# A mixture-of-experts decoder layer: expert rows weighted on their way out and added by the gathering DMA, gate and up weights one row to a packet

## The chip, the cores and the metric

The kernel runs on one core of one Trainium2 chip. The metric is device time in microseconds from one launch to its end. A profiled execution also gives a span, from its first to its last instruction. Everything is float32 at the interface; products are formed from two float32r parts (a rounded value and what the rounding left), in three matmuls each.

## The reference, cut to what matters

520 tokens (512 of a prompt, 8 samples) of 1024 numbers pass one layer: three convolution and gating branches, an output projection and a layer norm give `h`; then each token goes to two of 16 experts, and a second layer norm follows.

```python
def moe_ffn(h, ...):                     # 16 experts in 4 groups, the 2 best of the best group
    weights = sel_v / jnp.sum(sel_v, axis=-1, keepdims=True)
    gates = ...                          # (tokens, 16), two entries of each row not zero
    for e in range(N_EXPERTS):
        u = jax.nn.silu(t @ w_gate[e]) * (t @ w_up[e])      # (n,1024) @ (1024,512)
        out = out + gates[:, e:e + 1] * (u @ w_down[e])     # (n,512) @ (512,1024)
    return out.reshape(n, L, d)

f = moe_ffn(h, ...)
y = layer_norm(ALPHA * h + f, ln2_g, ln2_b)
```

The kernel divides by ALPHA throughout: it sums `h` and the two expert rows with weights over ALPHA, and takes the epsilon of the norm over ALPHA squared.

## The kernel before, in words

**Token mixer, 0 to 684 us.** `project` (L1079) multiplies 128-column blocks of weights, loaded 512 KB at a time (`raw`, L425) and split by ScalarE (L724) and GpSimd (L595). At the very start SyncE's queue loads inputs in a fixed order; `sb_tok`, the old state of a convolution, comes in at L439, and TensorE turns it at L1056 before it goes on.

**Opening of the experts, 684 to 733 us.** VectorE makes `h_tok` (L1712), SyncE stores it to `h_rows` in HBM, VectorE finds the two experts of each token and its place in the list of each. For an expert, `mark` (L1794) makes a one-hot matrix of tokens by places, `find_ids` (L1234) multiplies it with the token numbers, `take_ids` (L1801) makes them integers, GpSimd gathers up to 96 rows of `h_rows` into `hs` (L632), TensorE turns them (`turn`, L1245), ScalarE and VectorE make `hs_hi` (L891) and `hs_lo` (L1806). While the first gather runs TensorE turns the identity 18 times, and 8 times after the first `turn` (`keep_busy`, L1227).

**The expert stage, 733 to 988 us.** One step per expert, 16 in all, those of 1 to 12 in a hardware loop. Weights have three slots (expert e, e+1, e+2), 2 MB for each of gate, up and down. In a step TensorE does the gate product (24 matmuls of 512 columns), `find_ids` for the expert after the next, `turn_u`, `turn`, the up product (24) and the down product of the expert before (24), into `work[1]`. ScalarE rounds each of the 12 chunks into a ring of six, VectorE subtracts (`low_parts`, L1705). ScalarE's order in a step: up chunks, two down chunks, silu, `u_hi`, `hs_hi`, two down chunks, four gate chunks, and at the end `rows_out` (L900): it copies `work[1]` to `y_out` once the down product is done and the store of the last `y_out` has landed. VectorE's order: up chunks 0 and 1, `mark`, up 2 and 3, down 0 and 1, `take_ids`, `u_lo`, `hs_lo`, down 2 and 3, gate 0 and 1, `u`, gate 2 and 3. SyncE's queue issues, each after what it overwrites is used: gate of e+3, up of e+3, down of e+2 (all L474), and the store of `y_out` to `y_rows` (L483). All four go through one queue (q1) in this order; the gather of `hs` goes through GpSimd's (q0).

In HBM a row of gate or up is 512 floats, 2 KB. The view of before gives each partition two neighbouring rows (`e (j p i) f`, i=2), so that 4 KB are contiguous; the rows of the contraction are thereby paired, and `h_tok` is written with its columns in paired order (views `paired` and `plain`), `turn` takes its 128-column blocks in the order 0, 4, 1, 5, ..., and later sums with `h_back` go through the same views. Down has rows of 4 KB.

**The end, 960 to 1027.7 us.** In steps 13 and 14 VectorE works out at which row of `y_rows` the two results of each token lie (`find_slots`, `order_slots`, L1916 to L1935), the earlier-stored one first (`slot_early`, clipped to the first 12 experts). Once the down product of step 14 is done SyncE loads `h` back into `h_back`, and GpSimd gathers the earlier rows into `y_a` (L677). The last expert is split in halves (`up_last` L1289, `down_last` L1302). VectorE then spreads the samples' row numbers over the partitions (`spread_samples`, L1942 and L1943), makes the shares of the last expert (`share_marks`, L1952 to L1961) and forms `y_a*weight + h_back` (`partial`, L1967) for each of four token blocks and the samples. GpSimd gathers the later rows into `y_b` (`slot_ready`). The last expert's rows don't go through HBM for the prompt: TensorE adds identity times `y_a` (L1385) and three products of the weighted shares with the last rows (L1387) in PSUM. VectorE adds `y_b*weight` (L2006), with ScalarE (square, root, scale; L981, L984, L988) and GpSimd (add of the bias; L712) it normalises block after block, the samples between blocks 2 and 1, and five stores bring the results out.

GpSimd's queue at the end: four early gathers, the samples' early gather (after L1943), four late gathers (after L1961), the samples' late gather (after the last rows are stored), three bias adds.

Of the kernel before, what the change touches and what calls it, by code (L numbers as in the profile page):

```python
# [22 lines left out]
F32 = mybir.dt.float32  # L23
F32R = mybir.dt.float32r
BF16 = mybir.dt.bfloat16
I32 = mybir.dt.int32
# [90 lines left out]
def build(nc, x_prompt, x_sample, state_conv_a, state_conv_b, w_in, conv_a_w, w_a_out, conv_b_w, conv_b_bias,  # L117
# [4 lines left out]
    y_rows = nc.dram_tensor("y_rows", (PASSES * E * C, D), F32, kind="Internal").ap()  # L122
# [7 lines left out]
    gate_v = expert_w_gate[0].rearrange("e (j p i) f -> p (e j) (i f)", p=P, i=2)  # L130
    up_v = expert_w_up[0].rearrange("e (j p i) f -> p (e j) (i f)", p=P, i=2)
    down_v = expert_w_down[0].rearrange("e (k p) n -> p (e k) n", p=P)

    with ExitStack() as ctx:
# [103 lines left out]
        s_own, s_spread, s_idx = sb("s_own", [TS, 5]), sb("s_spread", [P, 5]), sb("s_idx", [P, 3], I32)  # L238
# [16 lines left out]
        share_tok = place("share_tok", "Q_HI", [P, 4, C], plus=NTB * D * 4)  # L255
        share_hi = place("share_hi", "Q_HI", [C, 4 * P], F32R, plus=NTB * D * 4 + 4 * C * 4)
        share_lo = place("share_lo", "Q_HI", [C, 4 * P], F32R, plus=NTB * D * 4 + 4 * C * 4 + 4 * P * 4)
        block_mean = place("block_mean", "acc_a", [P, P], plus=960)
        spread = place("spread", "acc_a", [TS, P], plus=960 + P * 4)
# [6 lines left out]
        onehot = place("onehot", "acc_a", [P, NTB, C], BF16)  # L266
# [9 lines left out]
        agg = sb("agg", [P, 2, 4])  # L276
        assert cursor[0] <= nc.sbuf_usable_end - 64, (cursor[0], nc.sbuf_usable_end)
# [47 lines left out]
        y_a_in, y_b_in = [sem(f"y_a_in{b}") for b in range(NTB)], [sem(f"y_b_in{b}") for b in range(NTB)]  # L325
        partial_ready = sem("partial_ready")
# [7 lines left out]
        class Pass:  # L334


            def __init__(self, tag):
                self.onehot_ready, self.ids_mm, self.ids_ready = sem(tag + "onehot"), sem(tag + "ids_mm"), sem(tag + "ids_ready")
                self.gathered = sem(tag + "gathered")
                self.turned, self.hs_hi_ready, self.hs_lo_ready = sem(tag + "turned"), sem(tag + "hs_hi"), sem(tag + "hs_lo")  # L340
# [44 lines left out]
        plain = lambda t: t.rearrange("p (g i) -> p i g", i=2)  # L385
        paired = lambda t: t.rearrange("p (i g) -> p i g", i=2)
        plain_s = lambda t: t.rearrange("p (x i) -> p i x", i=2)
        paired_s = lambda t: t.rearrange("p (i x) -> p i x", i=2)
        z_tile = (pr[0], work[1], pr[1], work[0])
        wide = lambda t: t.rearrange("p (h n) -> p h n", h=2)  # L390
        sz_in, sz = pr[0][:, 0, CS:2 * CS], pr[0][:, 0, 0:CS]
# [24 lines left out]
        def _(sp):  # L416
# [21 lines left out]
            load(0, N_S1 + 2, in_v, s1_roles[2])  # L438
            sp.dma_start(sb_tok[:], state_conv_b[0].rearrange("(b s) k n -> (s k) b n", b=2)).then_inc(states_in, 16)  # L439
# [30 lines left out]
            views = {"gate": (gate_v, KB // 2), "up": (up_v, KB // 2), "down": (down_v, FB)}  # L470
# [10 lines left out]
            def store(ps, e, t, row0):  # L481
                sp.wait_ge(ps.y_ready, t + 2)
                sp.dma_start(y_rows[bass.ds(e * C + row0, C), :], y_out[:]).then_inc(ps.stored, 16)  # L483

            def load_back():

                sp.dma_start(h_back[:, 0:4, :], h_rows[0:TP, :].rearrange("(b p) n -> p b n", p=P)).then_inc(back_in, 16)
                for i in range(2):
                    sp.dma_start(sh_back[:, i * (CS // 2):(i + 1) * (CS // 2)],
                                 h_rows[TP:T, :].rearrange("s (i c x) -> i s c x", i=2, x=CS // 2)[i]).then_inc(back_in, 16)  # L490
# [60 lines left out]
            with sp.If(n_max > C):  # L551
                sp.wait_ge(first.stored, 16 * E)
                sp.wait_ge(first.half_stored, 32)
                sp.wait_ge(partial_ready, NTB)
# [25 lines left out]
        def _(pool):  # L580
# [30 lines left out]
            pool.iota(e_off[:].rearrange("p b (g i) -> p b g i", i=PER_GROUP), pattern=[[0, NTB], [C, GROUPS], [GROUPS * C, PER_GROUP]], base=0, channel_multiplier=0, allow_small_or_imprecise_dtypes=True)  # L611
# [42 lines left out]
            pool.wait_ge(h_stored, 16 * NTB)  # L654
# [20 lines left out]
            def fetch(dst, slot, landed, table):  # L675
                for b in range(4):
                    pool.indirect_dma_start(out=dst[:, b, :], out_offset=None, in_=table,  # L677
                                            in_offset=bass.IndirectOffsetOnAxis(ap=slot[:, b:b + 1], axis=0)).then_inc(landed[b], 16)

            def fetch_samples(dst, which, landed, table):  # L680

                pool.indirect_dma_start(out=dst, out_offset=None, in_=table.rearrange("r (c f) -> (r c) f", f=CS),
                                        in_offset=bass.IndirectOffsetOnAxis(ap=s_idx[:, which:which + 1], axis=0)).then_inc(landed[4], 16)
# [6 lines left out]
            fetch_samples(sy_a, 0, y_a_in, y_rows[0:EARLY * C, :])  # L690
            n_max = further_passes(pool)
            with pool.If(n_max > C):
# [7 lines left out]
                fetch(y_a, slot_a, y_a_in, y_rows)  # L700
                fetch_samples(sy_a, 1, y_a_in, y_rows)
                fetch(y_b, slot_b, y_b_in, y_rows)
                fetch_samples(sy_b, 2, y_b_in, y_rows)
            with pool.Else():
                pool.wait_ge(slots_ready, 4)
                pool.wait_ge(first.stored, 16 * E)
                fetch(y_b, slot_ready, y_b_in, y_rows[0:(E - 1) * C, :])
                pool.wait_ge(first.half_stored, 32)
                fetch_samples(sy_b, 2, y_b_in, y_rows[0:E * C, :])
# [1391 lines left out]
```

## Time and profile before

| | us |
|---|---|
| three runs, median (lowest, highest) | 1028.82 (1028.72, 1029.62) |
| profiled execution | 1029.47 |
| its span | 1027.7 |
| TensorE busy in it | 999.9 (97%) |
| VectorE busy | 793.4 (77%) |
| ScalarE busy | 478.5 (47%) |
| GpSimd busy | 379.0 (37%) |
| mean granted TensorE clock | 0.993 |

Busy is the time in which an engine had an instruction in flight. A busy TensorE is not one at its peak, since matmuls are pipelined. The chain of waits goes back from the last instruction, at each step to what released it. DMA share is the time that the packets of the 16 DMA engines took, over 16 times the stretch; queues are SyncE's (q1), ScalarE's (q10) and GpSimd's (q0).

### The profile page before, as it was taken

Reading aid. Unit: us, or ns where it says so; the run is one execution under the profiler, and the core shown is the slowest. Engines: PE = TensorE matmul, PEld = TensorE weight load, DVE = VectorE, ACT = ScalarE, POOL = GpSimd, SP = SyncE. Lnnn points to the kernel's source line nnn. Section 1 sums busy time; section 2 is a strip of 40 time slices with the busy share of each in tenths; the row PEclk is TensorE's granted clock in tenths of the full one; section 3 lists DMA queues with packets and bytes.
Section 4 is the critical chain, followed back from the end, with each engine's and each line's share of the span. In section 5 each row is a group of like instructions: output and inputs, shape, how many; then the busy total and the mean of one; then the engine's idle time right before and its main releaser. Section 6 shows DMA issues by size and latency. Waiting matters only on the chain.

```text
span 1027.7 us, 19645 instructions
## 1 busy us (share of the span) xinstructions
PE 999.9 (97%) x7246; PEld 904.1 (88%) x7246; DVE 793.4 (77%) x982; ACT 478.5 (47%) x674; POOL 379.0 (37%) x278
## 2 busy tenths in 40 slices
PE   7999999999999999999999999998999999999995
PEld 7999999999999999999999999986677777777773
DVE  4598889888989985844434498237989898999987
ACT  4232322223232335134442323452788887878765
POOL 3444444444454755344544454320200000000355
PEclk9999999999999999999999999998999999999998
DMA  7432323233232222333235522647999999999475
GB/s 219 120 103 82 102 82 97 86 88 95 85 99 82 82 83 73 101 111 91 82 102 162 186 82 92 257 154 286 398 389 397 391 399 389 399 391 399 155 247 179
DMA packets 147290, 190.55 MB, mean 185 GB/s; under 512 B 6819, under 2 KB 114339, under 8 KB 147228
## 3 DMA queue, kind: packets, MB, share of 16 engines
q1 hardware_dynamic: 140107, 176.74, 49.4%
q0 software_dynamic: 3008, 10.55, 3.2%
q10 hardware_dynamic: 4129, 2.67, 0.9%
q8 instruction: 26, 0.43, 0.2%
q14 instruction: 20, 0.16, 0.1%
HBM read 179.16 MB, written 11.76 MB: 186 GB/s over the span
## 4 chain that ended last, share of the span: by engine, by line
PE 91%; DVE 5%; issue 2%; DMA 2%; ACT 1%; POOL 0%; SPq 0%; DVEq 0%; POOLq 0%; ACTq 0%
PE pr L1079 60%; PE pr L1269 16%; PE work L1269 8%; DMA sb_tok<-in_state_conv_b_dram 1%; PE work L1245 1%; PE work L1161 1%; PE pr L1310 1%; PE pr L1289 1%; DMA hs<-h_rows,ids 0%; PE work L1186 0%; DVE y_a L2015 0%; PE work L1087 0%; PE pr L1234 0%; DVE q_hi L1596 0%; PE pr L1178 0%
## 5 line engine op out<-in xcount | busy, mean ns | idle before, releaser
L595 POOL TENSOR_TENSOR w_lo<-raw,w_hi 128x512 fp32r<-128x512 f32 x208 | 297.2, 1449 | 326.8 <-ACT w_hi L724 326.8
L1079 PE MATMUL pr<-x_hi,w_hi 128*128 128x260 f32 x1264 | 255.2, 283 | 0.0
L1079 PE MATMUL pr<-x_hi,w_lo 128*128 128x260 f32 x1264 | 254.8, 283 | 0.0
L1079 PE MATMUL pr<-x_lo,w_hi 128*128 128x260 f32 x1264 | 254.3, 283 | 0.0
L728 ACT ACTIVATE ev<-pr 128x520 f32<-128x520 f32 x96 | 58.2, 606 | 372.7 <-PE pr L1079 372.7
L1079 PEld LDWEIGHTS pr<-x_hi,w_hi 128*128 128x128 f32 x1264 | 195.0, 189 | 0.3
L1079 PEld LDWEIGHTS pr<-x_hi,w_lo 128*128 128x128 f32 x1264 | 194.9, 188 | 0.0
L1079 PEld LDWEIGHTS pr<-x_lo,w_hi 128*128 128x128 f32 x1264 | 194.3, 188 | 0.0
L1522 DVE SCALAR_TENSOR_TENSOR work<-b_pad,par,work 128x512 f32<-128x512 f32 x224 | 148.1, 742 | 0.0
L724 ACT ACTIVATE w_hi<-raw 128x512 fp32r<-128x512 f32 x208 | 118.9, 622 | 3.7 <-DMA raw<-in_w_in_dram 3.4
L632 POOL DMA_INDIRECT hs<-h_rows,ids x15 | 19.3, 1288 | 247.5 <-DVE ids L1801 247.5
L1269 PE MATMUL pr<-ring,hs_hi 128*96 128x512 f32 x246 | 97.8, 398 | 0.0
L1269 PE MATMUL pr<-ring,hs_lo 128*96 128x512 f32 x246 | 96.8, 393 | 0.0
L1705 DVE TENSOR_TENSOR w_up_lo<-w_up,ring 128x1024 fp32r<-128x1024 f32 x64 | 75.2, 1219 | 19.0 <-ACT ring L868 19.0
L868 ACT ACTIVATE ring<-w_gate 128x1024 fp32r<-128x1024 f32 x64 | 67.8, 1062 | 23.3 <-PE pr L1269 10.6
L1705 DVE TENSOR_TENSOR w_down_lo<-w_down,ring 128x1024 fp32r<-128x1024 f32 x64 | 75.3, 1214 | 1.7 <-ACT ring L868 1.7
L1705 DVE TENSOR_TENSOR w_gate_lo<-w_gate,ring 128x1024 fp32r<-128x1024 f32 x64 | 75.4, 1215 | 0.8 <-ACT ring L868 0.7
L1582 DVE TENSOR_TENSOR ev<-ev,ev 128x520 f32<-128x520 f32 x16 | 11.9, 744 | 79.4 <-ACT ev L728 79.4
L868 ACT ACTIVATE ring<-w_down 128x1024 fp32r<-128x1024 f32 x64 | 65.7, 1053 | 4.7 <-PE pr L1269 4.0
L868 ACT ACTIVATE ring<-w_up 128x1024 fp32r<-128x1024 f32 x64 | 62.4, 1046 | 2.1 <-PE pr L1261 1.9
L1269 PEld LDWEIGHTS pr<-ring,hs_lo 128*96 128x96 f32 x246 | 39.7, 161 | 17.3
L1269 PEld LDWEIGHTS pr<-ring,hs_hi 128*96 128x96 f32 x246 | 39.8, 162 | 16.0
(397 smaller groups left out, 1749.7 us busy)
## 6 DMA issues: line engine op xcount, KB each, us to landing
raw<-in_w_in_dram SPq DMA_DIRECT2D x80, 512.0 KB, 3.7
w_gate<-in_expert_w_gate_dram SPq DMA_DIRECT2D x16, 2048.0 KB, 14.4
w_up<-in_expert_w_up_dram SPq DMA_DIRECT2D x16, 2048.0 KB, 13.0
w_down<-in_expert_w_down_dram SPq DMA_DIRECT2D x16, 2048.0 KB, 12.5
y_rows<-y_out SPq DMA_DIRECT2D x14, 384.0 KB
raw<-in_w_a_out_dram SPq DMA_DIRECT2D x8, 512.0 KB, 4.1
raw<-in_w_c_out_dram SPq DMA_DIRECT2D x8, 512.0 KB, 4.1
raw<-in_w_b_out_dram SPq DMA_DIRECT2D x8, 512.0 KB, 3.9
```

Of the source, the lines that this page charges most:

```text
L595: pool.tensor_tensor(w_lo[:, slot, k], raw[:, slot, k], w_hi[:, slot, k].bitcast(F32), ALU.subtract).then_inc(w_split, 1)
L632: pool.indirect_dma_start(out=hs[:], out_offset=None, in_=h_rows, in_offset=bass.IndirectOffsetOnAxis(ap=ids[:, m % 2:m % 2 + 1], axis=0)) ...
L724: act.activation(w_hi[:, slot, k], raw[:, slot, k], ACT.Copy).then_inc(w_rounded, 1)
L728: act.activation(out, src[:, :, 0:HALF], func).then_inc(evacuated, 1)
L868: act.activation(rounded(kind, i, last, opening, slots), chunk(kind, s, i), ACT.Copy).then_inc(ps.hi[kind], 1)
L1079: mm = pe.matmul(pr[slot][:, h, 0:HALF], w[:, slot, k, :], x[:, k, h * HALF:(h + 1) * HALF], start=(k == 0 and w is w_hi and x is hi), sto ...
L1161: mm = pe.matmul(work[TILE[f"sp{q}"]][:, i, c * P:(c + 1) * P], vt[:, c, g * P:(g + 1) * P], ws_t[:, g, :], start=True, stop=True)
L1245: mm = pe.transpose(work[0][:, k // 4, k % 4 * C:(k % 4 + 1) * C], source[:, (k % 2 * 4 + k // 2) * P:(k % 2 * 4 + k // 2 + 1) * P], ident ...
L1269: mm = pe.matmul(out(h), x[:, k, :], w[:, cols], start=(k == 0 and x is hi and w is w_hi_i), stop=(k == k_of * CH - 1 and x is lo))
L1522: do(dve.scalar_tensor_tensor(acc, b_pad[:, k:k + TP], col(j, R_CONVB + k), acc, ALU.mult, ALU.add))
L1582: do(dve.tensor_tensor(gate[:], gate[:], prod[:], ALU.mult))
L1705: dve.tensor_tensor(chunk(kind, s, i, w_e_lo), chunk(kind, s, i), rounded(kind, i, last, opening, slots).bitcast(F32), ALU.subtract).then_ ...
```

## The change

Five things are done together.

1. **Weights.** Gate and up are viewed as down is, one 2 KB row to a packet. `h_tok`, `turn` and the load of `h_back` go back to plain column order; the instructions stay as many.
2. **Gated rows.** Three more bf16 columns beside the token numbers hold each token's weight for each expert in three parts (`slot_cols`, made by the new `spread_weights` from nine small VectorE operations). `find_ids` multiplies five columns in place of two, from a place that a register gives. ScalarE sums the three parts of the gate into `gate` (`gate_in`), for the first two experts ahead of the first `hs_hi` (`first_gates`, after ten matmuls `find_gates` that take the place of the eight turns of the identity), for the others between `hs_hi` and down chunk 2 (`next_gate`, which waits for `take_ids`). `rows_out` and `last_rows_out` scale by it. `onehot` has two buffers.
3. **Adding gathers.** Both gathers of each block go straight into `h_back`, with the DMA adding; the early ones wait for the load of `h_back`, a late one for the early one of its block. A row of zeros (row 0 of `y_rows`, stored at the start behind the third weight load, ahead of `sb_tok`) serves where nothing is to be added. `partial`, `sample_partial` and a copy of the samples on ScalarE are gone.
4. **Shares.** They are plain ones and zeros: `share_marks` is one VectorE operation in step 14, the four turns stand in step 15 ahead of `up_last`, ScalarE copies them once (before the store of expert 14's rows), and `share_last` has two matmuls per half block in place of four. The low part of the last rows is made with the gate as a factor, and `y_last` is copied after it.
5. **Order.** `spread_samples` comes before the last chunk of `low_parts`; `order_slots` loses ten small operations and gains three (one clips, one multiplies, one makes `slot_ready`); the ScalarE root that loads a table moves behind the branch for further passes.

```diff
-    gate_v = expert_w_gate[0].rearrange("e (j p i) f -> p (e j) (i f)", p=P, i=2)
-    up_v = expert_w_up[0].rearrange("e (j p i) f -> p (e j) (i f)", p=P, i=2)
+    gate_v = expert_w_gate[0].rearrange("e (k p) f -> p (e k) f", p=P)
+    up_v = expert_w_up[0].rearrange("e (k p) f -> p (e k) f", p=P)
@@ SyncE, start
             load(0, N_S1 + 2, in_v, s1_roles[2])
+            sp.wait_ge(x_split, 1)
+            sp.dma_start(y_rows[0:1, :]..., b_pad[0:1, 0:16]...to_broadcast([1, D // 16, 16])).then_inc(h_stored, 16)
             sp.dma_start(sb_tok[:], ...).then_inc(states_in, 16)
@@ GpSimd, end
+            def fetch(b, slot, table):
+                pool.indirect_dma_start(out=h_back[:, b, :], out_offset=None, in_=table,
+                                        in_offset=..., compute_op=ALU.add).then_inc(y_in[b], 16)
             pool.wait_ge(slots_ready, 3)
             pool.wait_ge(first.stored, 16 * (EARLY + 1))
-            pool.wait_ge(first.done["down"], (E - 1) * CH)
-            fetch(y_a, slot_early, y_a_in, y_rows[0:EARLY * C, :])
-            pool.wait_ge(end_dve, 2)
+            pool.wait_ge(back_in, 32)
+            for b in range(4):
+                fetch(b, slot_early, y_rows[0:EARLY * C + 1, :])
+            pool.wait_ge(end_dve, 3)
...
                 pool.wait_ge(first.stored, 16 * E)
-                fetch(y_b, slot_ready, y_b_in, y_rows[0:(E - 1) * C, :])
+                for b in range(4):
+                    pool.wait_ge(y_in[b], 16)
+                    fetch(b, slot_ready, y_rows[0:(E - 1) * C + 1, :])
+                pool.wait_ge(y_in[4], 16)
                 pool.wait_ge(first.half_stored, 32)
@@ ScalarE
+            def gate_in(ps, src, m):
+                act.activation(gate_parts[:, m % 2], src, ACT.Copy, accum_out=gate[:, m % 6:m % 6 + 1]).then_inc(ps.gates_in, 1)
+            def next_gate(ps, m, t):
+                act.wait_ge(ps.ids_ready, t + 4)
+                act.wait_ge(ps.gates_in, t + 2)
...
-            def rows_out(ps, t):
+            def rows_out(ps, m, t):
                 act.wait_ge(ps.done["down"], t * CH + 2 * CH)
                 act.wait_ge(ps.stored, t * 16 + 16)
+                act.wait_ge(ps.gates_in, t + 1)
-                act.activation(y_out[:]..., work[1][0:C], ACT.Copy).then_inc(ps.y_ready, 1)
+                act.activation(y_out[:]..., work[1][0:C], ACT.Copy, scale=gate[:, m % 6:m % 6 + 1]).then_inc(ps.y_ready, 1)
@@ TensorE
                 turn(ps, n0)
-                if ps is first:
-                    keep_busy(8)
+                find_gates(ps, n0)
...
-                    pe.matmul(z_tile[b][:, h, :], ident[:], y_a[:, b, cols], start=True, stop=False)
-                    for w, y in ((share_hi, y_last_hi), (share_lo, y_last_hi), (share_hi, y_last_lo)):
+                    for y in (y_last_hi, y_last_lo):
@@ VectorE, end
-                    spread_samples()
-                    share_marks()
-                    partials(16)
+                    share_low(0)
+                    share_low(1)
```

## Rows read from the trace of the kernel before

**Rows 1.** The page: the chain of waits, shares of the span.

```profile
PE 91%; DVE 5%; issue 2%; DMA 2%; ACT 1%; POOL 0%; SPq 0%; DVEq 0%; POOLq 0%; ACTq 0%
```

**Rows 2.** A step: stretch, us, PE PEld DVE ACT POOL busy, clock, DMA share, GB/s.

```profile
930.00:948.00 18.00, 18.00 (x94) 12.95 (x93) 16.41 (x18) 14.67 (x17) 0.92 (x1) 1.00 1.03 396
```

**Rows 3.** DMA queues, 720 to 945 us: packets, MB, share of 16 engines.

```profile
q1 hardware_dynamic: 21161, 83.47, 95.0%
```

**Rows 4.** The same of 420 to 540 us, where rows are 512 B.

```profile
q1 hardware_dynamic: 20840, 11.47, 31.8%
```

**Rows 5.** The same of 1001 to 1007 us: two stores of 2 KB rows.

```profile
q10 hardware_dynamic: 224, 0.39, 19.8%
```

**Rows 6.** DMA issues, 745 to 762 and 923 to 941: KB, us to landing.

```profile
w_gate<-in_expert_w_gate_dram SPq DMA_DIRECT2D x1, 2048.0 KB, 14.4
...
w_gate<-in_expert_w_gate_dram SPq DMA_DIRECT2D x1, 2048.0 KB, 14.9
```

**Rows 7.** Tile y_rows: DMA to landing, us.

```profile
DMA to landing us min/median/max: 2.1/5.7/12.1
```

**Rows 8.** Timeline, SyncE and ScalarE: start us, us [idle before <-releaser].

```profile
942.76 0.36 SPq L483 DMA_DIRECT2D y_rows<-y_out  x1
...
959.35 1.03 ACT L900 ACTIVATE y_out<-work 96x1024 f32<-96x1024 f32 x1 [1.70 <-PE work L1269]
```

**Rows 9.** Timeline of one step, VectorE and TensorE.

```profile
785.03 0.65 DVE L1794 TENSOR_TENSOR onehot<-ev,router 128x480 bf16<-128x480 f32 x1
786.01 0.34 PE L1234 MATMUL pr<-id_cols,onehot 128*96 128x2 bf16 x5
790.14 0.15 DVE L1801 TENSOR_REDUCE ids<-pr 96x1 int32<-96x2 f32 x1
```

**Rows 10.** The chain of waits at the start: start us, us, what.

```profile
15.22 0.39 SPq L425
15.65 11.39 DMA sb_tok<-in_state_conv_b_dram
```

**Rows 11.** Timeline of the opening, TensorE, ScalarE, VectorE.

```profile
711.96 1.14 PE L1245 MATMUL work<-ident,hs 96*128 96x96 f32 x8 [0.24 <-DMA hs<-h_rows,ids]
713.14 0.81 ACT L891 ACTIVATE hs_hi<-work 128x768 fp32r<-128x768 f32 x1 [8.51 <-PE work L1245]
714.00 0.48 PE L1257 MATMUL pr<-ring,hs_hi 128*96 128x512 f32 x1
708.91 0.16 DVE L1801 TENSOR_REDUCE ids<-pr 96x1 int32<-96x2 f32 x1
```

**Rows 12.** Timeline of ScalarE: a small operation that sums.

```profile
1016.31 0.31 ACT L1001 ACTIVATE y_b<-pr,s_agg 128x64 f32<-128x64 f32 x1
1016.52 0.19 ACT L1001 ACTIVATION_READ_ACCUMULATOR y_b<-pr,s_agg 128x1 f32 x1
```

**Rows 13.** Timeline of the end, VectorE.

```profile
1000.39 0.17 DVE L1961 CAST slot_ready<-s_pos 128x5 int32<-128x5 f32 x1
1006.76 1.29 DVE L2006 SCALAR_TENSOR_TENSOR pr<-y_b,s,pr 128x1024 f32<-128x1024 f32 x1 [0.82 <-PE pr L1387]
1008.22 1.27 DVE L1967 SCALAR_TENSOR_TENSOR y_a<-y_a,s,h_back 128x1024 f32<-128x1024 f32 x1
1014.44 0.29 DVE L2038 SCALAR_TENSOR_TENSOR pr<-y_b,s_spread,pr 128x64 f32<-128x64 f32 x1
```

**Rows 14.** Timeline of the end, ScalarE and its queue: the last rows.

```profile
1002.55 0.58 ACT L912 ACTIVATE y_last_hi<-work 96x512 fp32r<-96x512 f32 x1
1002.68 0.32 ACTq L914 DMA_DIRECT2D y_rows<-y_last  x1
```

**Rows 15.** Timeline of the end, GpSimd's gathers of the later rows.

```profile
1000.83 1.74 POOL L677 DMA_INDIRECT y_b<-y_rows,slot_ready  x1 [0.82 <-DVE slot_ready L1961]
1008.30 2.02 POOL L682 DMA_INDIRECT y_b<-y_rows,s_idx  x1 [0.30 <-issue]
```

**Rows 16.** Tile slot_ready: DMA to landing, us.

```profile
DMA to landing us min/median/max: 5.5/5.7/5.9
```

More of the change, by code:

```diff
@@ L265, in build @@
         u_lo = place("u_lo", "par", [P, FB, C], F32R)
-        onehot = place("onehot", "acc_a", [P, NTB, C], BF16)
+        onehot = [place(f"onehot{i}", "acc_a", [P, NTB, C], BF16, plus=i * NTB * C * 2) for i in range(2)]
+        slot_cols = place("slot_cols", "rw", [P, NTB, E, 5], BF16)
         iota = ev[4][:, 0:C]
@@ L553, in _ @@
                 sp.wait_ge(first.half_stored, 32)
-                sp.wait_ge(partial_ready, NTB)
+                for b in range(NTB):
+                    sp.wait_ge(y_in[b], 16)
                 sp.wait_ge(end_mm, 6)
@@ L699, in _ @@
                 pool.wait_ge(y_read, 1)
[L700 to L703, printed above, removed]
+                pool.wait_ge(back_in, 64)
+                for b in range(4):
+                    fetch(b, slot_a, y_rows)
+                fetch_samples(1, y_rows)
+                for b in range(4):
+                    pool.wait_ge(y_in[b], 32)
+                    fetch(b, slot_b, y_rows)
+                pool.wait_ge(y_in[4], 32)
+                fetch_samples(2, y_rows)
             with pool.Else():
@@ L940, in step @@
                         rounded_parts(ps, "up", s, uses[s] + m // 3, t, slots="down")
-                        rows_out(ps, t - 1)
+                        rows_out(ps, m - 1, t - 1)
+                        if ps is first:
+                            act.wait_ge(end_mm, 1)
+                            act.activation(share[:], pr[1][0:C, 1, :], ACT.Copy).then_inc(end_act, 1)
                         return
@@ L1342, in step @@
                         down(ps, (m - 1) % 3, t - 1, slots="up")
+                        if ps is first:
+                            pe.wait_ge(end_dve, 2)
+                            for b in range(4):
+                                mm = pe.transpose(pr[1][0:C, 1, b * P:(b + 1) * P], share_tok[:, b, :], ident[:])
+                            mm.then_inc(end_mm, 1)
                         pe.wait_ge(ps.u_ready, t * 2 + 2)
@@ L1351, in step @@
                     if m <= 13:
-                        find_ids(ps, t + 2)
+                        find_ids(ps, m, t + 2, expert(2))
                     if m:
@@ L1838, in expert_pass @@
                 take_ids(ps, 1, n0 + 1)
+                if ps is first:
+                    spread_weights()
                 if ps is further:
```

282 lines of the change are left out of this document (128 added, 154 removed).

## The prediction

> **What bounds the kernel now.** First the page's chain of waits: TensorE's own work is 91% of the span [rows 1], so what does not reach TensorE costs nothing until the end. Then the busy time by stretch: an expert's step takes 17.9 us, TensorE has no gap in it, ScalarE 3.3 us and VectorE 1.6 us of 18; the DMA engines have none either, 396 GB/s at a share of 1.03 [rows 2]. So two resources are full at the same pace. That the DMA engines are just at their limit shows in the landings: gate loads take 14.4 us from issue to landing at 745 us and 14.9 at 923 [rows 6], though 2 MB at 396 GB/s are 5.3; the queue is never empty and its backlog grows a little. Third, the cover: gate, up and down are loaded two to three steps ahead, some 38 us between issue and use against 15, so they may be late by 20 us. The store of `y_out` stands in the same queue behind them, and its cover is short: issued at 942.76, it has to have landed when ScalarE writes the next `y_out` at 959.35 [rows 8], 16.6 us later. Of the landings that the view shows for `y_rows` the longest is 12.1 us [rows 7]; I take it for a store of this stage. 16.6 - 12.1 leaves 4.5 us. Last, the chain at the start goes through the load of `sb_tok` [rows 10], in the opening through the first gather, the turn, `hs_hi` and then TensorE without a pause [rows 11], and at the end through VectorE.
>
> **Weights in 2 KB packets.** As many bytes in twice the packets: 2 MB in 1024 in place of 512. What a packet costs: in the expert stage 16 x 225 us x 0.950 / 21161 = 161.6 ns at a mean of 3945 B [rows 3]; in the mixer 16 x 120 x 0.318 / 20840 = 29.3 ns at 550 B [rows 4]. The line through both is 7.8 ns + 0.039 ns per byte: 2 KB cost 88 ns, twice that is 175 against 167 for 4 KB. A load has 512 more packets on 16 engines, 32 each, 0.25 us. The only 2 KB packets in the trace are two stores beside gathers: 16 x 6 x 0.198 / 192 = 99 ns (the 224 hold 32 completion writes) [rows 5]; by them a load would cost 32 x (2 x 99 - 167) = 1.0 us more. The bounds are 0 and 1.0; I take 0.30, by the line, since loads are its kind, with a little for packets that meet others. Steps issue no slower, so the backlog grows by 0.60 us a step. From the moment the queue was last empty (713.9) to the store at 942.76 there are 26 loads of gate or up: 7.8 us. The cover takes 4.5, passed after some 15 loads, in step 8. From there on `y_out` waits for its store, and behind it on ScalarE stand the up chunks, behind those on VectorE `mark`, and for that TensorE's `find_ids` waits: `mark` ends at 785.68 and TensorE begins at 786.01 [rows 9], a cover of 0.3. So the last steps run at the pace of the DMA engines, and the stage ends 7.8 - 4.5 - 0.3 = 3.0 us later. With 0.16 per load or less nothing shows; with 0.45 it is 6.9; a cost of 1.0 would give 21, which I don't reach for, since a write beside gathers is the farther row.
>
> The Trainium skill, "DMA: Bandwidth & Descriptors", section Specifications, puts the least transfer for line rate at 512 B; by this 2 KB would cost what 4 KB do per byte. The trace disagrees at 512 B: 29.3 ns for 550 B is 301 GB/s over 16 engines, 161.6 for 3945 is 391 [rows 3, 4]. By the rule this term would be 0 and the sum 1029.0; that is the first rival below.
>
> **Gates in the steps.** `find_ids` has as many matmuls, three columns wider: 0.34 us as now. It takes its place from a register, which adds sequencer instructions to TensorE; no row shows their cost there. They run ahead under 5.5 us of products unless `mark` is late; bounds 0 and 0.1 a step (12 steps, 1.2 us), taken 0. `next_gate` on ScalarE costs an operation and a read of the sum: 16.52 - 16.31 + 0.19 = 0.4 us [rows 12], and it waits for `take_ids`, done at 790.29 [rows 9]; behind it stand two down chunks and four gate chunks, with 3.3 us of ScalarE's slack in the step [rows 2], and VectorE behind those with 1.6. They are used by TensorE 3 us later or more, so 0. The scale from a tile in `rows_out` adds some 0.1 us in the tight loop of `mark`; taken 0, it is in the 0.3 above.
>
> **Start.** SyncE issues one more DMA before `sb_tok`; one costs its queue 0.39 us and 0.04 between [rows 10], and `x_split` has long come. `sb_tok` is waited for by TensorE from its landing at 27.04 on, after which TensorE never waits in the mixer: +0.4 us (0, if the DMA engines, loaded then, hide it, to 0.8).
>
> **Opening.** `first_gates` stands ahead of the first `hs_hi`, which began 0.04 us after the turn, and TensorE began 0.05 us after that [rows 11]. New before it: ten small matmuls, 2 x 0.18 = 0.35 us (five of them span 0.34 with their tail [rows 9]), and two gate sums, 2 x 0.4 = 0.8 [rows 12]. `spread_weights` has nine small operations, some 2.5 us from 709.07, and is done before the turn ends at 713.1. The eight turns of the identity ran beside `hs_hi` and free nothing. +1.1 us, 0.8 to 1.6; TensorE paces what follows, so it stays.
>
> **End.** Gone from VectorE: three partials before the last products and, between the first two sums, the fourth (1.27 us [rows 13]) and the samples' (0.3). Gone from TensorE: eight identity products and a third of the others; the first sum waited 0.82 us for TensorE at 1006.76 [rows 13]. `slot_ready` no longer comes last, at 1000.39 [rows 13]; instead the late gathers wait behind the samples' early one, whose row numbers come at about 998.5, so the first is issued at 1000.0 in place of 1000.83 [rows 15]. At 5.7 us to landing [rows 16] the first sum begins at 1005.7, 1.0 earlier, and the second 2.6 earlier. Against this: the four turns of shares ahead of `up_last` (0.35), ScalarE's copy of them ahead of the down chunks (0.6), for which VectorE was already waiting, and `spread_samples` ahead of the last chunk (0.3) push the last rows back by 1.2; the second half no longer waits for the shares and gains as much. But each half is now rounded (0.58 [rows 14]), waits for its low part, and is then copied: its store goes out at about 1004.3 in place of 1002.68 [rows 14]. It lands near 1008, and only then may the samples' late gather be issued, as late as now, 1008.30 [rows 15]. It lands at 1012 to 1014 (4 to 5.7 us after). Before it stand the first three sums, done by 1011.7, and behind it blocks 1 and 2 and the sum of block 3. That sum was at 1014.44 [rows 13] and comes at 1012.5: -1.9 us, if an adding gather is as fast as a copying one. If an adding packet takes twice the time, a gather of 512 KB takes 2.6 us of all engines in place of 1.3, the four late ones land at 1006.4, 1009, 1011.6 and 1014.2, the samples after them at 1014.9, and the end comes 0.5 later than now. No row shows an adding DMA. Bounds -2.5 and +2; I take -1.1, between the two, as nothing is near.
>
> The Trainium skill, same page, section "Rules for kernel authors", says that an accumulating DMA reads its destination and writes it later. No run here shows it; that is the doubled case, by which the end would be +0.5 in place of -1.1 and the sum 1.6 us higher.
>
> **Sum.** 3.0 + 0 + 0.4 + 1.1 - 1.1 = +3.4 us on a profiled execution of 1029.47, which lay 0.65 above the median. On the median of 1028.82 that is 1032.2.
>
> **Rivals.**
> - *The backlog stays hidden; not slower.* A load costs 0.16 us more or less, or the growth is taken up as loads of the queue are issued later. For it: a packet's own cost is the smaller part of 88 ns, and mean packet times at a share of 1.03 hold queueing. Against: landings grow already [rows 6], so no room is left. Then 0 + 0.4 + 1.1 - 1.1: 1029.2.
> - *The end gives more, and the backlog is hidden; faster.* The mechanism is VectorE's chain at the end: the samples' gather lands by 1011.5, adding costs nothing, and all of 1.0 + 1.5 us is kept. It decides if that gather lands before the third sum ends. 1028.82 + 1.5 - 2.8 = 1027.5, and 1026.4 if the opening costs but half.
> - *Adding gathers are dear.* Late gathers queue behind each other at 2.6 us and VectorE waits for each. 3.0 + 1.5 + 0.5 to 2: 1033.8 to 1035.3. For it: two early gathers of a block in a row, each reading what it adds to. Against: the engines are nearly idle at the end.
> - *Packets are dearer.* 0.45 us a load: 6.9 in place of 3.0, 1036.1.
> - *The change doesn't do what it says*, the 2 KB rows being joined to larger packets: then it is the first rival.
>
> **How the numbers follow.** Forecast 0.37, its own range 1030.9 to 1034; backlog hidden 0.22 (about no change); faster end 0.16; dear gathers 0.13; dear packets 0.12. The range leaves out the ends of the last two and a part of the third: 1026.8 to 1036. A measurement here tells 0.2%, 2.1 us, from no change: faster means below 1026.8, 0.15; within, to 1030.9, 0.30; slower 0.55.
>
> **What would show it.** Right: in the expert stage packets of q1 double in number at 85 to 95 ns; landings of gate loads grow from about 15 us to over 20 and `y_out` gets an idle time released by a DMA in the last third, while steps go from 17.9 to 18.4 us there. `sb_tok` issued at 16.1; the first product of the experts 1.1 us further from the turn. At the end VectorE waits before the samples' sum. Wrong: steps of 17.9 us throughout with the store's landing under 16 us, or steps of over 18.4 from the start of the stage; a step that waits for `find_ids` or `hs_lo` with the store long landed; gathers that land later than 8 us after issue.

## The result, and the profile after

The changed kernel takes 1042.78 us (median of 4 runs, 1041.97 to 1044.09) against 1029.22 for the kernel before beside it; the ratio is 1.0133, 95% interval 1.0115 to 1.0150. It is 13.6 us slower; the forecast was +3.4, its range ended at +7.2. The profiled run took 1041.97 (span 1040.1).

Both traces are cut at three marks that every kernel here has: VectorE's last `m` of the mixer, TensorE's turn of `u` in step 1 and in step 15, and the end of VectorE's last operation. Each number is a difference of start times in the chain of waits or the timeline.

| stretch | before | after | |
|---|---|---|---|
| start to the end of the mixer | 683.37 | 682.41 | -1.0 |
| opening, to the turn of `u` in step 1 | 49.31 | 51.49 | +2.2 |
| steps, to the turn of `u` in step 15 | 247.05 | 251.93 | +4.9 |
| end, to VectorE's last operation | 43.77 | 51.54 | +7.8 |

That is 13.9; the spans differ by 12.4, as the last stores behind that mark took 1.5 less.

**Steps.** The chain of waits of the kernel after, in step 2 of the loop and in step 13, which stands outside it and takes its columns from a fixed address (start us, us, what):

```profile
751.66 0.56 PE pr L1263 x5
752.22 0.46 PE pr L1348 x4
...
953.12 0.19 PE pr L1263 x5
953.31 0.39 PE pr L1348 x4
```

And what stands in TensorE's queues for that line in the whole stage (ns min/median/max):

```profile
L1263 PEldq FUSED_REGOPS  x60: 46/46/84, 733.1 to 935.0; - x60
```

L1263 is `find_ids`. In the loop its five products take 0.50 to 0.56 us and the turn of `u` behind them 0.46; outside, with the same five columns, 0.19 and 0.39. That is some 0.43 us in each of the twelve steps whose address comes from a register, and steps of 18.31 us in place of 17.88. The 60 register operations are one to a product, 5 in each of the 12 steps; in the step above they start from 751.3 to 751.9 us, among the weight loads of the five products, which span 0.67 us there and 0.41 in step 13. So they are not done ahead, under the products before. The stretch of a step, the DMA queue of 720 to 945 us and what ScalarE waits for before it writes `y_out` (all 15 times TensorE), beside [rows 2, 3, 8]:

```profile
930.00:948.00 18.00, 18.00 (x89) 12.92 (x88) 16.31 (x17) 14.23 (x19) 0.92 (x1) 1.00 1.04 386
```
```profile
q1 hardware_dynamic: 33314, 81.41, 96.6%
```
```profile
  PE work L1307: 26.9, 15
```

Packets grew from 21161 to 33314, and GB/s fell from 396 to 386, but `y_out` never waited for its store: the forecast's main term did not appear. The slower steps gave the DMA engines the time they needed; e1 below bears that out.

**Opening.** The chain, and the granted clock of three stretches (its column stands third from the end), against [rows 11]:

```profile
710.99 0.88 PE work L1283 x8
711.87 0.42 PE pr L1272 x10
...
712.32 0.41 ACT gate_parts L905 x4
712.73 0.71 ACT hs_hi L898
...
713.48 0.74 PE pr L1295
714.22 0.43 PE pr L1296
```
```profile
711.00:713.00 2.00, 1.28 (x18) 1.19 (x18) 0.00 (x0) 0.68 (x5) 0.00 (x0) 1.00 0.19 76
713.00:715.00 2.00, 1.52 (x4) 1.07 (x5) 1.54 (x2) 0.43 (x1) 0.00 (x0) 0.52 0.59 74
715.00:717.00 2.00, 2.00 (x7) 1.30 (x6) 2.00 (x3) 0.54 (x1) 0.00 (x0) 0.62 0.97 352
```

`find_gates` and the gate sums stand in the chain as forecast. Behind `find_gates` TensorE was idle from 712.3 to 713.5, and then the granted clock fell to the level of 1.2 GHz: the first products take 0.43 us each, and 0.23 where it is 2.4.

**End.** GpSimd's gathers, VectorE, and ScalarE around its branch, against [rows 13 to 16] (start us, us, engine line, operation, [idle before <- releaser]):

```profile
994.72 2.39 POOL L675 DMA_INDIRECT h_back<-y_rows,slot_early  x1 [30.96 <-DMA h_back<-h_rows]
...
1006.80 1.54 POOL L675 DMA_INDIRECT h_back<-y_rows,slot_ready  x1 [0.30 <-issue]
...
1019.46 1.55 POOL L680 DMA_INDIRECT h_back<-y_rows,s_idx  x1 [5.57 <-DMA y_rows<-y_last]
```
```profile
1015.90 1.23 DVE L2015 SCALAR_TENSOR_TENSOR pr<-pr,h_back 128x1024 f32<-128x1024 f32 x1 [5.62 <-DMA h_back<-y_rows,slot_ready]
...
1030.93 1.23 DVE L2048 SCALAR_TENSOR_TENSOR y_b<-h_back,s_agg 128x64 f32<-128x64 f32 x1
...
1032.26 2.19 DVE L2051 SCALAR_TENSOR_TENSOR y_a<-y_b,s_agg,h_back 128x64 f32<-128x64 f32 x1
1034.38 1.28 DVE L2023 SCALAR_TENSOR_TENSOR work<-work,agg,ln_rows 128x1024 f32<-128x1024 f32 x1
```
```profile
1011.04 0.32 ACTq L938 DMA_DIRECT2D y_rows<-y_last  x1
1020.84 1.28 ACT L1049 ACT_TABLE_LOAD   x1 [9.83 <-issue]
```

And the DMA queues and landings of 1003 to 1018 us:

```profile
q0 software_dynamic: 843, 2.58, 93.8%
...
y_rows<-y_last ACTq DMA_DIRECT2D x2, 192.0 KB, 7.3
h_back<-y_rows,slot_ready POOLq DMA_INDIRECT x4, 10.6
```

Three things to see. The late gathers land after 10.6 us in place of 5.7, with the DMA engines full at only 200 GB/s. ScalarE issues nothing for 9.8 us around its branch (2.9 before). Two operations of VectorE on 64 columns take 1.23 and 2.19 us. The forecast had the first as its doubled case, worth 1.6 us; the other two had no term.

Which of them paces the end is in the chain of waits (start us, us, what):

```profile
1010.32 0.69 ACT y_last L936
...
1013.70 7.14 issue
1020.84 1.28 ACT L1049
...
1023.54 1.29 DVE y_a L2023
```

It goes from the last rows over ScalarE's branch to its first square, and from there along VectorE; no gather stands in it. The first square starts 36.4 us after the turn of `u` in step 15, 29.1 before: with the 2.0 us of the two operations (e6) that is more than the whole loss. So in the changed kernel the adding gathers wait in the shadow of the branch, and come out once that is repaired (e5, e8).

### The profile page after: what moved, and what is told of

Same layout as the page of the kernel before. It is cut to its first block, busy times and chain, and to the rows that moved or that the text cites. A ratio compares the mean times of both kernels' runs of the same rounds, so it can differ in the third digit from the quotient of the medians.

```text
span 1040.1 us, 19719 instructions
## 1 busy us (share of the span) xinstructions
PE 997.2 (96%) x7224; PEld 903.7 (87%) x7224; DVE 791.7 (76%) x969; ACT 476.6 (46%) x703; POOL 366.4 (35%) x278
## 4 chain that ended last, share of the span: by engine, by line
PE 91%; DVE 4%; issue 3%; ACT 1%; DMA 0%; ACTq 0%; POOL 0%; DVEq 0%; POOLq 0%
PE pr L1107 60%; PE pr L1307 16%; PE work L1307 8%; PE work L1283 1%; PE pr L1263 1%; PE work L1189 1%; PE pr L1348 1%; PE pr L1126 1%; PE pr L1327 1%; DMA hs<-h_rows,ids 0%; PE work L1214 0%; DVE y_a L2023 0%; PE work L1115 0%; DVE q_hi L1634 0%; PE pr L1206 0%
## 5 line engine op out<-in xcount | busy, mean ns | idle before, releaser
L631 POOL DMA_INDIRECT hs<-h_rows,ids x15 | 13.9, 929 | 260.1 <-DVE ids L1852 247.0
```

The costliest lines, as they stand in the source:

```text
L631: pool.indirect_dma_start(out=hs[:], out_offset=None, in_=h_rows, in_offset=bass.IndirectOffsetOnAxis(ap=ids[:, m % 2:m % 2 + 1], axis=0)) ...
```

## The experiments

Times are medians; the kernel before lay at 1028.6 to 1029.0 beside them. A median carries some scatter of the start: the end of the mixer lies between 682.4 and 683.5 in the profiles, but at 685.6 in those of e1 and e5, where TensorE waited 1.8 and 1.7 us for `sb_tok` (0.7 before, at most 1.3 in the other kernels) and its first 16 products behind it took 2.4 and 2.6 us in place of 1.9 (granted clock 0.65 and then 0.50 from 28 to 31 us in e5). So what each experiment shows is read by stretch. The end scatters too: e1 and e7 change nothing in it and have 49.4 and 50.0 against the 51.5 of after. That is the gap at ScalarE's branch: its first square starts 34.2 and 34.9 us after the turn of `u` in place of 36.4, and the ends are shorter by just that. So there a difference of 2 us says nothing by itself, and the place is read in the trace:

| kernel | time | opening | steps | end |
|---|---|---|---|---|
| before | 1028.7 | 49.31 | 247.05 | 43.77 |
| after | 1042.8 | 51.49 | 251.93 | 51.54 |
| e1 fixed tile of columns | 1037.1 | 50.37 | 247.46 | 49.36 |
| e2 before, 2 KB packets | 1030.5 | 49.04 | 247.55 | 43.89 |
| e3 gathers that copy | 1039.3 | 50.43 | 252.26 | 48.98 |
| e4 root ahead of the branch | 1041.6 | 50.49 | 252.25 | 50.04 |
| e5 branch turned round | 1042.6 | 50.57 | 251.76 | 48.58 |
| e6 samples in PSUM | 1041.4 | 51.89 | 251.91 | 48.38 |
| e7 gate sums late | 1040.0 | 49.80 | 251.85 | 50.02 |
| e8 = e1, e5, e6, e7 | 1033.8 | 49.46 | 247.35 | 48.08 |
| e9 = e8, late gathers copy | 1031.2 | 50.52 | 248.71 | 43.25 |
| e10 = e9, 4 KB, strided turn | 1033.8 | 50.19 | 251.44 | 42.79 |

(In e7, e9 and e10 the turn of step 15 is not in the chain and is taken from the timeline.)

**e1: is it the register?**

```
+ dve.tensor_copy(cols_now[:, m % 2], slot_cols[:, :, bass.ds(x, 1), :]...)      # in mark
- of = slot_cols[:, b, bass.ds(x, 1), :]                                         # in find_ids
+ of = cols_now[:, m % 2, b, :]
```

> After, but VectorE copies the five columns of the expert to a fixed tile beside each mark, and TensorE reads that tile instead of an address from a register. Theory (the register addresses cost TensorE its 0.43 us a step): find_ids back from some 0.5 to 0.2 us in the chain of waits, looped steps from 18.31 to about 17.9, the time 4 to 5.5 us under the changed kernel's 1042.8, so 1037 to 1039. Rival A (the steps are paced by the DMA engines, which move 2 KB packets): steps stay at 18.3, 1042.8. Rival B (the wider product, five columns for two, costs): find_ids stays at 0.5. A mixture that I keep open: steps are 17.9 at first and longer in the last third, where y_out waits for its store, as forecast: then 1040 to 1041.

1037.08 (1036.36 to 1038.90). The chain of the same step:

```profile
753.63 0.19 PE pr L1266 x5
753.82 0.39 PE pr L1351 x4
754.20 0.66 PE work L1286 x8
```

Five columns from a fixed address take 0.19 us, and the steps 4.5 us less. The register address is shown as the cause; width and DMA are ruled out. The time is at the lower end of what was expected. The mixture came too, smaller: `y_out` waited five times for its store and two late steps were 17.97 and 18.05 us.

**e2: the packets alone.** The kernel before, with the two views and their counts changed. It leaves out the plain column order of the tokens that goes with them, so its output is another; the work is the same:

```
- "e (j p i) f -> p (e j) (i f)", i=2
+ "e (k p) f -> p (e k) f"
```

> Before, with only the gate and up matrices loaded one 2 KB row to a packet (the rows then meet the wrong columns of the tokens, the work is the same). The recorded term: 0.30 us a load, backlog of 7.8 us by step 14, stage 3.0 us longer, so 1032.2. Rival A (a packet of 2 KB costs half of one of 4 KB, or the queue has more cover than I counted): no change, 1029.2 and steps of 17.88 to the end. Rival B (packets dearer): 1036.

1030.47 (10 runs, 1029.28 to 1032.76), ratio 1.0016, interval 1.0006 to 1.0025. What `y_out` waits for and how its store lands, and one piece of the chain of waits:

```profile
  PE work L1269: 15.6, 9
  DMA y_rows<-y_out: 12.5, 6
...
DMA to landing us min/median/max: 3.2/15.7/16.3
```
```profile
925.26 16.29 DMA y_rows<-y_out
```

The mechanism is the one forecast: the landing grows step by step (13.0, 13.6, 14.5, 15.0, 15.8 us for the first five stores), stops at about 16 when it meets the cover, and from 869 us on, in step 8, ScalarE waits for the store, which stands in the chain from 925. But it costs 0.5 us in the steps, 1.7 by the medians (the profiled execution, 1029.28, was the fastest of the ten), not 3.0. The queue q1 held 33550 packets at 97.2% of 225 us, 104.3 ns each; less some 7650 of 4 KB (12.6 steps of 512 and 96) at the 161.6 ns of [rows 3], a 2 KB packet took 87 to 88 ns. That is the 88 of the forecast's line; what the forecast added above it ("a little for packets that meet others") was not there. By 32 x (2 x 87.5 - 167) = 0.26 us a load the forecast's own sum gives 26 x 0.26 - 4.8 = 2.0 us, still four times the 0.5 of the trace; what holds the rest back is not shown.

**e3: is adding dear?** The ten gathers overwrite, which leaves `h` and the earlier rows out of the sums:

```
- ..., compute_op=ALU.add)
+ ...)
```

> After, with the ten gathers of rows overwriting in place of adding (the sums then lack the residual and the early rows; all else the same). Theory (adding is dear for the DMA engines, some twice a copy): late gathers land 5.5 to 6 us after issue in place of 10.6, the DMA engines are under a share of 0.6 from 1003 to 1023, the first sum starts 4 us earlier, and ScalarE's gap of 9.4 us at the branch falls to about 3 as before, since what it waits for there comes over the same DMA engines; 1042.8 less 3 to 5: 1038 to 1040. Rival (the gap at the branch comes from the place of the square root's table load): gap unchanged, end 0 to 2 us earlier.

1039.27 (1038.42 to 1040.59). The same 15 us:

```profile
q0 software_dynamic: 781, 2.73, 54.9%
...
h_back<-y_rows,slot_ready POOLq DMA_INDIRECT x4, 6.4
```

The first sum starts at 1011.25 in place of 1015.90. Per packet 16 x 15 x 0.549 / 781 = 169 ns where adding took 16 x 15 x 0.938 / 843 = 267; from 1013 to 1015 us the engines moved 371 GB/s at a share of 0.94, the adding ones 217 at 1.07. Adding is shown as dear. The Trainium skill, "DMA: Bandwidth & Descriptors", section "Rules for kernel authors", has an accumulating DMA read its destination and write it later; the trace fits it, with little over half the rate. The part on ScalarE's gap fell: it is 7.3 us here (9.8 after), so most of it is not the adding, and VectorE, its sums done early, waits 5.6 us (3.1 after) for ScalarE's first square. That starts 2.6 us nearer to the turn of `u`, which is all that the end is shorter by: on the chain of the changed kernel the adding costs nothing beyond what it may add to the gap.

**e4 and e5: the gap at the branch.** e4 puts `act.activation(r_tok..., Sqrt)` ahead of it; e5 turns it round:

```
- with act.If(n_max > C): <further passes>
- with act.Else(): act.nop()
- <root>; normalised()
+ with act.If(n_max < C + 1): <root>; normalised()
+ with act.Else(): <further passes>; <root>; normalised()
```

> After, with ScalarE's small Sqrt that loads the table put back ahead of the branch. Theory of contention: the branch still takes its 7 us beside the adding gathers, what follows it comes 0 to 1.3 us earlier; 1042.8 less 0 to 1.3. Rival (the table load behind the branch is what waits, or brings the wait about): ScalarE's Square starts 5 us or more earlier than 1022.3, VectorE's normalise(0) loses its wait of 3.1 us; 1040 to 1041.

> After, with ScalarE's branch turned round: what follows it in this input (root and normalising) stands directly behind the branch, the code of the further passes behind that. Theory (the 6 to 7 us between the branch and the next instruction are the fetch of instructions from a far place, over the DMA engines that are busy with the gathers): the gap falls from 7.1 to under 2 us, ScalarE's first Square comes 5 us earlier, VectorE no longer waits 3.1 us for it; the time 1.5 to 3 us under 1042.8. Rival (the branch waits for the value it loads, or for anything that comes wherever the code stands): gap and time unchanged.

e4: 1041.57 (1040.46 to 1043.64), 1.2 less as contention allows, but within the scatter; the root's table load came at 1011.39, a gap of 5.7 us stood behind the root, and the first square started 2.4 us earlier, not the 5 of the rival. e5: 1042.58 (1041.40 to 1043.34), ScalarE first, then the chain of waits:

```profile
1013.09 0.32 ACTq L938 DMA_DIRECT2D y_rows<-y_last  x1
1014.56 1.28 ACT L1042 ACT_TABLE_LOAD   x1 [1.50 <-issue]
```
```profile
1013.09 7.89 DMA y_rows<-y_last
...
1021.73 4.14 DMA h_back<-y_rows,s_idx
```

The gap went from 9.8 to 1.5 us with nothing changed but the order of the code: it belongs to the jump over the further passes. The traces speak for instructions fetched by the DMA engines: two queues of the kind `instruction` (q8 and q14) move packets of 16 KB and less, and in each of the eight long gaps (before, after, e1 to e4, e6, e7) at least one of them does, the last some 1 to 2 us before the gap ends (after: at 1019.4, the gap to 1020.8; before: at 1005.9, to 1007.5). In the gaps of 1.0 to 1.6 us of e5, e8, e9 and e10 there is none. The gap was also longer where the DMA engines were busier (2.9 us before, 7.3 in e3, 9.8 after). That these packets are ScalarE's instructions no view says. VectorE's wait of 3.1 us for ScalarE's first square is gone, yet the time missed what was expected, 1.5 to 3 us less. In the profiled execution the end is 3.0 us shorter and the mixer ended 3.2 later; where the three others lost it isn't known. At the end the next chain comes out: the store of the last rows, 7.9 us to landing, and the samples' gather behind it.

**e6: VectorE behind GpSimd.**

```
+ act.activation(sz, sh_back, ACT.Copy)                      # sz, sz_out: PSUM
- scalar_tensor_tensor(sy_b, sh_back, ...); scalar_tensor_tensor(sy_a, sy_b, ...)
+ scalar_tensor_tensor(sz_out, sz, ...);    scalar_tensor_tensor(sy_a, sz_out, ...)
```

> After, with the samples' two last VectorE operations reading their first operand from PSUM (a copy that ScalarE makes) in place of SBUF. Theory (VectorE, with both operands in SBUF, is held until GpSimd's running addition ends): the operations of 128x64 fall from 1.23 and 2.19 us to 0.3 each, as before, and the last normalising starts 2.9 us earlier, less what ScalarE's own chain for block 3 allows; 1042.8 less 1.5 to 3. Rival (the operations are long for another reason, as the memory of h_back or the DMAs): unchanged.

1041.36 (1040.82 to 1043.53):

```profile
1030.83 0.28 DVE L2050 SCALAR_TENSOR_TENSOR pr<-pr,s_agg,h_back 128x64 f32<-128x64 f32 x1
...
1031.21 0.28 DVE L2053 SCALAR_TENSOR_TENSOR y_a<-pr,s_agg,h_back 128x64 f32<-128x64 f32 x1
1032.25 1.29 DVE L2025 SCALAR_TENSOR_TENSOR work<-work,agg,ln_rows 128x1024 f32<-128x1024 f32 x1 [0.76 <-ACT y_b L1012]
```

Shown. In the kernel after, GpSimd's first two additions ran from 1026.36 for 2.35 us and from 1029.72 for 2.36, the next followed; VectorE's operations ended at 1032.16 and 1034.45, when the second and the third addition did. The Trainium skill, "SBUF — State Buffer", section "Who interferes with whom", says that a VectorE instruction with two SBUF inputs contends with a GpSimd instruction that reads SBUF, and calls the lock on the shared ports exclusive. The trace agrees, 0.28 against 1.23 and 2.19 us. From the first of the two to the last normalising it is 1.42 us in place of 3.45, so 2.0 of the expected 2.9, as ScalarE's `y_b` then ends last. The time, 1.4 less, is just short of the 1.5 to 3 expected.

**e7: the gate sums.** `first_gates` moves from ahead of step 0 to behind `tokens_in(ps, 0, t)`.

> After, with the two first gate sums of ScalarE behind hs_hi in place of ahead of it. Theory (they stand on the chain of the opening): the first product comes 0.41 us (the part of them that the chain shows) to 0.8 us nearer to the turn, the time 0.4 to 0.8 less, 1042.0 to 1042.4, in the profile and hardly beyond what a median tells. Rival: TensorE's clock decides there: the granted clock falls where TensorE has a long pause before the first product, and the time moves by 1.2 either way.

1040.04 (1038.82 to 1041.02). The chain:

```profile
711.19 1.01 PE work L1283 x8
...
712.22 0.82 ACT hs_hi L898
...
713.08 0.47 PE pr L1295
```

The time is 2.7 less, beyond the 0.4 to 0.8 expected. The opening is 1.7 us shorter than after's: the gates' 0.7 (as e3 and e4, whose clock stayed up, stand to it) and 1.0 of a granted clock that is 1.00 from 713 on; the end, which this edit leaves alone, is 1.5 shorter, as the gap at ScalarE's branch is. The clock fell behind the pause in after and e6 (1.2 us) and in e9 (0.5), and not in e1, e3, e4 and e5 (1.2) nor in e7 and e8 (0.5); what decides isn't settled, so the 1.0 is not something that this edit is shown to give back. Another 0.4 of the opening is step 1's `find_ids`.

**e8: together.**

> After with the fixed tile of columns, the branch turned round, the samples' operands in PSUM and the late gate sums together. If the parts add up: 1042.8 - 5.7 - 2 - 2.5 - 0.5 = 1032. If they share one chain at the end (the store of the last rows, 7.2 us to landing, then the samples' gather, 5.6 us, both beside adding gathers), the two at the end give 2 together and it is 1034.5.

1033.80 (1031.86 to 1034.83): between the two values expected, 0.7 below the one of a shared chain. Opening and steps are as before, and the end is still 4.3 us longer, on one chain:

```profile
1004.66 8.79 DMA y_rows<-y_last
...
1014.20 4.23 DMA h_back<-y_rows,s_idx
```

The late gathers are close behind that chain: VectorE waits 5.4 and 2.5 us for them ahead of its first two sums, and only 0.8 for the samples.

**e9: the late gathers copy.**

```
- indirect_dma_start(out=h_back[:, b, :], ..., slot_ready, compute_op=ALU.add)     # waits for the early one
+ indirect_dma_start(out=y_b[:, b, :], ..., slot_ready)
+ pe.matmul(z_tile[b][:, h, :], ident[:], h_back[:, b, cols], start=True, stop=False)
+ act: y_last[h], its store, then y_last_hi[h]
```

> The kernel with all four repairs (e8), and at the end: the late gathers copy into a tile of their own, waiting for no early one, TensorE adds residual and early rows by a product with the identity, and ScalarE writes and stores each half of the last rows before it rounds it. Theory (what is left of the end, 4.3 us from the last turn of u to the end, is the adding gathers: two in a row for a block, at half rate, and beside them the store of the last rows, 8.8 us to landing, and the samples' gather, 4.2): the store lands within 5 us, the first sum starts 2 us or more earlier, the end falls from 48.1 to 43 to 45 us, the time to 1028 to 1030.5, about that of before. Rival (the end is bound by VectorE and TensorE, whatever the gathers do, or the identity products, some 7 us of TensorE, take their place): 1033 to 1034.

1031.24 (8 runs, 1028.82 to 1033.03), ratio 1.0023, interval 1.0012 to 1.0033. VectorE's first sum, and the landing of the last rows:

```profile
1011.21 1.23 DVE L2030 SCALAR_TENSOR_TENSOR pr<-y_b,pr 128x1024 f32<-128x1024 f32 x1 [4.65 <-DMA y_b<-y_rows,slot_ready]
```
```profile
DMA to landing us min/median/max: 5.5/5.8/6.1
```

The end is 43.25, 0.5 less than before, so what was left of the loss lay in the two things that this edit changes. One is the adding of the late gathers: the second sum starts 30.0 us after the turn of `u` in place of e8's 34.0. The other is ScalarE's order: the second half of the last rows is stored 22.6 us after it in place of 25.3 (before: 23.0). Their shares were not measured apart. The store lands after 5.8 us, not within the 5 expected, and the time misses its range by 0.7; the steps are 1.7 longer than before's (the store again, twice in the chain, 16.4 and 16.2 us to landing) and the clock of the opening fell.

**e10: large packets, strided turn.** The views of before in e9, and in `turn`:

```
- source[:, k * P:(k + 1) * P]
+ source.rearrange("c (j q i) -> c j i q", i=2, q=P)[:, k // 2, k % 2, :]
+ keep_busy(8)                                              # behind find_gates
```

> The kernel before this one (e9) with gate and up in packets of 4 KB again, the gathered rows turned from every second column so that the products stay right, and the eight turns of the identity back behind find_gates. Theory (what e9 lost in the steps, 1.6 us, is the store of y_out waiting in a queue of 2 KB packets; the turn does not care which columns it reads): steps of 17.9 to the end, no wait for the store, the eight operations of the turn at 0.7 us as before, and no granted clock of 1.2 GHz after the first product; 1031.2 less 1.3 to 2.5: 1028.7 to 1030. Rival (the packets cost nothing, or the strided turn costs what they give back): 1031.

1033.76 (1032.82 to 1034.27):

```profile
752.27 0.96 PE work L1290 x8
```
```profile
DMA to landing us min/median/max: 3.2/10.9/11.2
```

The time is outside both values expected. The store lands after 10.9 us throughout and nothing waits, as the theory has it; but steps of 18.31 us hid the 2 KB packets too (after), so this run does not tell the packets from its slower steps. With the eight turns of the identity the granted clock is 1.00 from 711 on. The other half fell: eight turns of every second column take 0.96 us, of adjacent ones 0.66, since loading such a block as weights takes TensorE 216 ns in place of 140, and each step is 18.19 us. Columns stored in the weights' order, as the kernel before has them, allow both large packets and quick turns. No version beat the kernel before.

## Why the prediction was wrong, by its steps

Two steps failed: the gates in the steps, put at 0, and the end, whose path was another. By the marks +13.9 stands against +3.4; of the 10.5 between them gates in the steps are 5.2, the end 8.9, the opening 0.7, the packets -3.0 and the start -1.4, which leaves 0.1.

- **Gates in the steps, "bounds 0 and 0.1 a step (12 steps, 1.2 us), taken 0".** The largest single cause that the runs isolate. Measured 0.43 a step, 5.2 us over twelve (e1 gives 0.41 a step back). The argument was that sequencer work runs ahead under the products; the trace has a register operation to each of the five short products, done among their weight loads. The bound itself was wrong: no row of before held a register address on TensorE, and 0.1 was no row's number.
- **Weights in 2 KB packets, +3.0.** In the changed kernel 0, since the term above hid it. Alone 0.5 in the trace and 1.7 by the ratio, 0.6 to 2.6 (e2). The mechanism and the cap at the cover were right; the size was too large. That the waits began in step 8, as forecast, is partly luck: the landing of 12.1 us from which the cover of 4.5 was worked out is that of the second early gather, issued at 983.28, and the trace of before has no landing of a `y_out` store at all. (For no cost of the packets the prediction gives the sum as 1029.0 once and 1029.2 once; it is 1029.2.)
- **Start, +0.4.** -1.0 in the profile of after, and -0.9 to +0.1 in the others, e1 and e5 (+2.2) aside, so no cost of the added DMA is seen.
- **Opening, +1.1.** 0.7 of gates, as the sums overlap; and 1.0 of granted clock in the profiled run, which the forecast left out ("The eight turns of the identity ran beside `hs_hi` and free nothing"). Without them TensorE pauses there, and behind that pause the clock fell in three of nine kernels.
- **End, -1.1, "Bounds -2.5 and +2".** The largest miss in size. +7.8 in the profile, 5.6 to 7.8 by the kernels that leave the end as it is (e1, e7). The path was wrong: the forecast had VectorE's sums and the samples' gather pace the end; the chain goes over the jump of ScalarE, behind which the change puts the root, and after it VectorE is held by GpSimd's additions, since the samples' operands are no longer in PSUM. Neither had a term. The adding gathers are the next path (e5, e8). Their doubled case was the right one, but it was priced alone: the early gathers could start only when `h_back` had landed (994.72; the forecast kept before's place), so that adding at half rate filled the DMA engines from there to 1021 and each landing there grew, that of the last rows from 3.1 to 7.3 us. The last rows' second store also went out 2.3 us later against the turn of `u` (25.2 after it, 23.0 before), where the forecast had 1.6. Two repairs together leave 4.3 (e8), since each uncovers the next wait; with the late gathers copying and the last rows stored before they are rounded all of it is gone (e9).
- **Rivals.** "Adding gathers are dear" named what comes out of the end once ScalarE's jump is repaired, with 0.5 to 2 us of queueing, against it that "the engines are nearly idle at the end": the adding gathers themselves filled them. "Backlog hidden" came true for a reason it did not name. No rival had TensorE's own step grow.

## What to carry to other kernels

On the engine that sets the pace, an address from a register can have a price even behind long work (here 0.43 us for five short products): let an engine with slack copy the slice to a fixed place. A DMA that adds is to be priced with its dependencies: what it adds to must have landed, the next one on it must wait, and what runs beside it lands later (here a store of 192 KB after 7.3 us in place of 3.1). Code that is taken after a branch belongs right behind it (a gap of 1.5 us in place of 9.8). And a stage that gains slack elsewhere can hide a cost that comes back when the first loss is repaired (the 2 KB packets here), so costs are best measured alone.

## What the runs showed of the hardware that was not expected

- Five products of TensorE with an address from a register: 0.50 to 0.56 us, with a fixed one 0.19, and the four turns behind them 0.46 against 0.39. A register operation of 46 ns goes with each product.
- A jump over a long piece of code on ScalarE: 2.9 us before, 5.7 to 9.8 in the kernels with busier DMA engines, 1.0 to 1.6 where the code taken stands next.
- Gathers that add took 267 ns a packet, gathers that copy 169.
- VectorE with both operands in SBUF was held until GpSimd's running addition ended (1.23 and 2.19 us for 64 columns); with one in PSUM it was not (0.28).
- Turning every second column of a float32 tile costs 0.96 us for eight, adjacent columns 0.66.
